# The stretch between two feed-forward blocks as one pipeline over tiles, with the window means as products on TensorE

## What is computed

```python
x = x + gate_f * rmsnorm_2(conv_ffn(h, w_up[0], ...), g_post_ffn[0])      # layer 0 ends
h = modulate(rmsnorm_2(x, g_pre_mix[1]), shift_m, scale_m)                # layer 1: h * (1 + scale) + shift
# multiscale_pool_mix: four groups of 256 channels, windows w = 2, 4, 8, 16 tokens
lo = jnp.clip(t - w // 2, 0, L); hi = jnp.clip(t + (w - w // 2), 0, L)
pooled = (csum[hi] - csum[lo]) / (hi - lo) - hg                           # window mean less the token itself
y = jnp.einsum('blgc,gce->blge', pooled, w_pool) + b_pool
y = y.reshape(B, L, D_MODEL) * pool_scale
x = x + gate_m * rmsnorm_2(y, g_post_mix[1])
h = modulate(rmsnorm_2(x, g_pre_ffn[1]), shift_f, scale_f)                # input of the second conv_ffn
```

## Time and profile before

| | |
|---|---|
| median of 3 runs | 4270.84 us (4269.49 to 4272.86) |
| the profiled execution's own time | 4271.75 us |
| its span, first to last instruction | 4269.8 us |
| mean granted TensorE clock | 0.914 of full speed |
| busy share: PE, PEld, DVE, ACT, POOL | 84%, 74%, 55%, 29%, 34% |

### The profile page before, as it was taken

How to read it: one execution, slowest core, us unless ns; L and a number is a source line. 1 busy time by engine, 2 the same in 40 slices (tenths; PEclk the granted TensorE clock), 3 DMA queues, 4 the chain that set the end, 5 groups by cost and what they waited for, 6 DMA issues and landing times. The chain is left out here.

```text
span 4269.8 us, 60179 instructions
## 1 busy us (share of the span) xinstructions
PE 3587.3 (84%) x19351; PEld 3162.1 (74%) x19351; DVE 2357.5 (55%) x4928; ACT 1228.9 (29%) x2747; POOL 1443.9 (34%) x1814
## 2 busy tenths in 40 slices
PE   5899877999998876757997769999994239999996
PEld 4799666999998865647886658888883238888885
DVE  6477664666777753126775244445445764444545
ACT  2255112656554521103432131112112022111111
POOL 3354322555665434431111342222213352222221
PEclk8899878999999978878998879999997569999998
DMA  4210544111111141100000021111101111111112
GB/s 163 80 39 17 222 182 156 39 40 58 56 58 54 33 170 49 40 11 1 0 0 30 10 99 44 59 44 44 45 28 40 40 69 59 53 50 44 44 44 79
DMA packets 67132, 255.69 MB, mean 60 GB/s; under 512 B 7328, under 2 KB 34208, under 8 KB 53920
## 3 DMA queue, kind: packets, MB, share of 16 engines
q1 hardware_dynamic: 66976, 253.79, 16.6%
HBM read 219.95 MB, written 33.82 MB: 59 GB/s over the span
## 5 line engine op out<-in xcount | busy, mean ns | idle before, releaser
L1777 PE MATMUL ps<-hT_hi,up_hi 128*128 128x512 f32 x1408 | 549.7, 390 | 15.0 <-DVEq L1730 15.0
L1778 PE MATMUL ps<-hT_lo,up_hi 128*128 128x512 f32 x1408 | 549.2, 390 | 0.0
L1779 PE MATMUL ps<-hT_hi,up_lo 128*128 128x512 f32 x1408 | 548.9, 390 | 0.0
L1681 POOL TENSOR_TENSOR up_lo<-up_raw,up_hi 128x2048 fp32r<-128x2048 f32 x42 | 194.5, 4630 | 866.6 <-ACT up_hi L1702 866.6
L1740 DVE TENSOR_TENSOR x<-ps,x 128x512 f32<-128x512 f32 x704 | 457.1, 688 | 2.1 <-PE ps L1793 2.1
L293 PE MATMUL ps<-w_hi,hT_hi 128*128 128x512 f32 x848 | 337.4, 398 | 70.2 <-DVE hT_lo L317 35.0
L294 PE MATMUL ps<-w_lo,hT_hi 128*128 128x512 f32 x848 | 335.6, 396 | 0.0
L295 PE MATMUL ps<-w_hi,hT_lo 128*128 128x512 f32 x848 | 335.3, 395 | 0.0
L545 PE MATMUL ps<-identity,rows 128*128 128x128 f32 x464 | 104.2, 417 | 273.3 <-DVE rows L441 254.8
L1777 PEld LDWEIGHTS ps<-hT_hi,up_hi 128*128 128x128 f32 x1408 | 265.2, 188 | 70.9 <-POOLq L1629 15.8
L1779 PEld LDWEIGHTS ps<-hT_hi,up_lo 128*128 128x128 f32 x1408 | 265.2, 188 | 55.3
(11 more groups left out here) (233 smaller groups left out, 8376.8 us busy)
## 6 DMA issues: line engine op xcount, KB each, us to landing
mod_weights<-in_w_mod SPq DMA_DIRECT2D x24, 2048.0 KB, 8.4
up_raw<-in_w_up SPq DMA_DIRECT2D x44, 1024.0 KB, 4.8
down_raw<-in_w_down SPq DMA_DIRECT2D x44, 512.0 KB, 5.6
w_raw<-in_w_in_b SPq DMA_DIRECT2D x24, 768.0 KB, 4.4
x_kept<-x SPq DMA_DIRECT2D x3, 4096.0 KB, 15.7
group_rows<-unit_rows SPq DMA_DIRECT2D x64, 132.0 KB, 1.8
unit_rows<-group_rows SPq DMA_DIRECT2D x64, 132.0 KB, 2.1
x<-in_x SPq DMA_DIRECT2D x2, 4096.0 KB, 15.6
```

What stands on the lines that cost most here:

```text
L1777: nc.tensor.matmul(out, a, t_hi[:, k, cols], start=(k == 0), stop=False)
L1778: nc.tensor.matmul(out, a, t_lo[:, k, cols], start=False, stop=False)
L1779: last = nc.tensor.matmul(out, b, t_hi[:, k, cols], start=False, stop=(k == KT - 1))
```

## The change

All blocks listed above, from the residual of layer 0 to the columns of the second `conv_ffn`, become one block, `PoolMix`, written out over 22 slots. In slot i an engine handles tile i - lag for each of its steps, so that up to eight tiles are in flight at different steps. The lags on VectorE are: scale with 1/rms (1), add the old row (2), scaled rows `h` (3), copy of half the pooled columns (6), scale of the mixed rows (8), residual (9), normed rows (11), `lo` columns (13).

The window means become products: for a tile and a group of 128 channels TensorE multiplies the tile's own rows with a 128x128 band matrix (the inverse counts, less the identity), and adds the last 64 rows of the tile before and the first 32 rows of the tile behind, with matrices from a new input `windows`. The result comes out with channels on the partitions, which is what the product with `w_pool` wants; the first `turn` is gone. The bias is a float32r product over 64 partitions (bias `hi` in row 0, `lo` in row 32, zeros elsewhere), `pool_scale` is multiplied into `w_pool` once. The mean of squares goes to ScalarE (Identity with scale 1/1024 and bias eps), so GpSimd has one small instruction per 1/rms and not two. Shift and gain of the last turn are one ScalarE instruction per 128 columns (eight a tile); the shift of `h` stays a GpSimd add. The factors and rows that were made by `rows_of_product` and `gained` are made once, after the second mixer, by `keep_rows`: seven small instructions of VectorE, one transpose, one copy, one DMA to a DRAM tensor, from which each is loaded by a broadcasting DMA. `X` is stored to `x_kept` tile by tile. Both `conv_ffn` are unchanged, and so is all before them.

```diff
+class PoolMix:
+    SLOTS = TILES + 14
...
+    def sync(self, sp):
+        sp.dma_start(self.old[:, 0], self.kept[:, 0]).then_inc(core.ready0.sem, 16)
+        sp.dma_start(self.old[:, 1], self.kept[:, 1]).then_inc(core.ready1.sem, 16)
+        sp.wait_ge(core.row_vectors.sem, core.row_vectors.at(16))
+        sp.dma_start(self.f_post[:], self.rows[0].partition_broadcast(P)).then_inc(core.post_row.sem, 16)
+        for dst, row in ((self.p_row, self.rows[1]), (self.s_row, self.rows[2])):
+            sp.dma_start(dst[:], row.partition_broadcast(P)).then_inc(core.pre_rows.sem, 16)
+        for dst, src in ((self.B[:], I["windows"]), (self.w[:], I["w_pool"]), (self.e_row[:], I["pool_scale"].partition_broadcast(P)),
+                         (self.b_row[:], I["b_pool"].partition_broadcast(P)), (self.f_mix[:], self.rows[3].partition_broadcast(P))):
+            sp.dma_start(dst, src).then_inc(core.constants.sem, 16)
+        self.ahead.first_loads(sp)
+        for m in range(2, TILES):
+            sp.wait_ge(core.x_new.sem, core.x_new.at(m - 1))
+            sp.dma_start(self.old[:, m % 2], self.kept[:, m]).then_inc((core.ready0, core.ready1)[m % 2].sem, 16)
+        for m in range(TILES):
+            sp.wait_ge(core.x_next.sem, core.x_next.at(m + 1))
+            sp.dma_start(self.kept[:, m], self.X[:, m]).then_inc(core.x_kept.sem, 16)
...
+    def tensor(self, pe):
+        for i in range(self.SLOTS):
+            m = self.tile_at(i, 6)
+            if m is not None:
+                if m == 0:
+                    pe.wait_ge(core.constants.sem, core.constants.at(16 * 5))
+                pe.wait_ge(core.h_rows.sem, core.h_rows.at(min(m + 2, TILES)))
+                for half, used in ((0, core.pooled_act), (1, core.pooled_dve)):
+                    pe.wait_ge(used.sem, used.at(m))
+                    for k in range(4 * half, 4 * half + 4):
...
+                        last = nc.tensor.matmul(out, H[:, m % 5, cols], B[:, g, 0 if m == 0 else 2 if m == TILES - 1 else 1],
+                                                start=True, stop=not (before or behind))
+                        if before:
+                            last = nc.tensor.matmul(out, H[P // 2:P, (m - 1) % 5, cols], B[P // 2:P, g, 3], start=False, stop=not behind)
+                        if behind:
+                            last = nc.tensor.matmul(out, H[0:P // 4, (m + 1) % 5, cols], B[0:P // 4, g, 3], start=False, stop=True)
+                    last.then_inc(core.pooled.sem, 1)
+            m = self.tile_at(i, 11)
...
+            m = self.tile_at(i, 7)
...
+                    nc.tensor.matmul(bank, self.one[:], self.bias[:, half * 512:half * 512 + 512], start=True, stop=False)
+                    for g in (2 * half, 2 * half + 1):
                         for k in range(2):
...
+                            last = nc.tensor.matmul(bank[:, (g % 2) * 256:(g % 2) * 256 + 256], self.d[:, m % 2, 2 * g + k], self.w[:, g, k],
+                                                    start=False, stop=(k == 1 and g % 2 == 1))
...
+        def square(n, m, src):
...
+            act.activation(self.junk[:, len(used) % 2], src, ACT.Square, accum_out=self.ss[:, n, m:m + 1]).then_inc(done[n].sem, 1)
...
+            act.activation(self.rs[:, n, m:m + 1], self.ss[:, n, m:m + 1], ACT.Identity, scale=1.0 / D, bias=core.eps[:]).then_inc(mean[n].sem, 1)
...
-        feed_forward(0)
...
-            turn(core, TILES, Stage(core, x_rows(X)), scale=pre[:], shift=mod[1][:, 0:8], plain=h)
-            pool_windows(core, h, I["inverse_counts"])
...
+                pool_mix(PoolMix(core, st2, T, T_at, up_at, X, x_dram, rows_dram, I, pre_ffn[:], mod[1][:, 24:32], up_weights))
+            feed_forward(1, T, up_weights)
```

More of the change, by code:

```diff
@@ L2043, in rows_of_product @@
     core.turned.passed(1)
[L2048 to L2104, removed]
@@ L2142, with pool_mix @@
+def pool_mix(mix):
+    with mix.core.nc.Block() as block:
+        block.sync(mix.sync)
+        block.gpsimd(mix.gpsimd)
+        block.scalar(mix.scalar)
+        block.vector(mix.vector)
+        block.tensor(mix.tensor)
+    mix.passed()
 VECTORS = {}
@@ L2363, in build @@
-        if stop == "e":
-            return ended()
-        feed_forward(1, lambda m: out[0, m * P:(m + 1) * P, :])
+        with ExitStack() as st:
+            T = split_columns(st)
+            gained(core, pre[:], vcol("g_pre_ffn", 0), mod[0][:, 32:40])
+            up_weights = UpWeights(core, st, I["w_up"][0])
+            turn(core, TILES, Stage(core, x_rows(X)), T, scale=pre[:], shift=mod[0][:, 24:32], ahead=up_weights, kept=(x_dram, X[:]))
+            feed_forward(0, T, up_weights)
+        with ExitStack() as st:
+            T_at = nc.sbuf_base
+            T = split_columns(st)
+            up_at = nc.sbuf_base
+            up_weights = UpWeights(core, st, I["w_up"][1])
+            with ExitStack() as st2:
+                pool_mix(PoolMix(core, st2, T, T_at, up_at, X, x_dram, rows_dram, I, pre_ffn[:], mod[1][:, 24:32], up_weights))
+            feed_forward(1, T, up_weights)
@@ L2368, in tile_part @@
+        with ExitStack() as st:
+            factor = core.sb(st, "factor", [P, D])
+            rows_of_product(core, vcol("g_post_ffn", 1), mod[1][:, 40:48], factor[:])
+            add_normed(core, x_tile, factor[:], x_tile, old=lambda m: x_dram[:, m], result=lambda m: out[0, m * P:(m + 1) * P, :])
 def tile_part(Z):
@@ L2416, in constants @@
     masks = np.stack([np.where(np.stack(p, 1), f(0), f(BIG)) for p in pairs]).astype(f)
[L2417 to L2420 removed]
+    windows = np.zeros((4, len(t), len(t)), f)
+    for g, w in enumerate((2, 4, 8, 16)):
+        lo, hi = np.clip(t - w // 2, 0, len(t)), np.clip(t + w - w // 2, 0, len(t))
+        inside = (t[:, None] >= lo) & (t[:, None] < hi)
+        windows[g] = np.where(inside, f(1) / (hi - lo).astype(f), f(0)) - np.eye(len(t), dtype=f)
+    first, mid, last = ((m * P, (m + 1) * P) for m in (0, 1, TILES - 1))
+    beside = np.zeros((4, P, P), f)
+    beside[:, P // 2:] = windows[:, P + P // 2:2 * P, 2 * P:3 * P]
+    beside[:, :P // 4] = windows[:, 2 * P:2 * P + P // 4, P:2 * P]
+    windows = np.stack([windows[:, a:b, a:b] for a, b in (first, mid, last)] + [beside], 1).transpose(2, 0, 1, 3)
+    return {"rotary": rotary, "axial": axial, "masks": masks, "windows": windows,
             "identity": np.eye(P, dtype=f)}
```

328 lines of the change are left out of this document (270 added, 58 removed).

## The result

The changed kernel takes **4205.4 us** (median of 4 runs, 4197.5 to 4208.3) against 4271.3 for the kernel before (median of 4 runs beside it): a ratio of 0.984 with a 95% interval of 0.983 to 0.986. It is 66 us faster. The prediction was 4146, 125 faster, with a range up to 4186. The sign was right, and the time lies 19 us above the range.

What follows compares the result with a forecast made beforehand. No engine was full; the chain of blocks bounded the stretch. Filling 27, TensorE 97.6, emptying 19, block ends 1.2 and `keep_rows` 5 made 149.8 against 274.6 us, so 4270.84 - 124.8 = 4146.0 us, range 4122 to 4186.

Steps and rivals of the forecast that it cites:

- The bare work: TensorE's products and transposes for the eight tiles of the new block, at full clock: 74.7 us.
- The changes of height: TensorE switching between products over 128, 64 and 32 rows: 192 changes at 0.08 us, 15.4 us (0 to 31.3).
- Half clock: TensorE starting its phase at half clock after being idle: some 2.5 us.
- Rival (d): TensorE stays at half clock through its phase, 180.3 us in place of 97.6: total 4229 us; chance 0.13.
- Waits of the first tiles: In TensorE's phase, first tiles wait for each other, as window products need the tile behind: 5 us.
- (b): Each change of height on TensorE breaks the overlap in full, 31.3 us: 16 more, total 4162 us; chance 0.14.
- Filling: Start of the stretch until TensorE's first product, behind 7.5 MB of queued transfers: 27 us.
- Emptying: The last mixed tile's way through the remaining steps to the end: 19 us, middle of 14.3 and 24.
- Rival (c): VectorE and GpSimd hold each other up, pace 13.1 us a tile: 11 more, total 4157 us; chance 0.14.
- Rival (e): Slots don't overlap as written; an in-order loop lets one tile through per 22.6 us: total 4229 us; chance 0.05.
- (a): No change of height on TensorE costs anything and the tail is bare: total 4126 us; chance 0.10.
- (f): At half clock each change of height also exposes a weight load, 0.61 us each: slower, 4315 us; chance 0.02.

Runs made afterwards that it cites:

- experiment 1: The changed kernel with all window and bias products over 128 rows, missing rows filled with zeros: 4143.2 us, ratio 0.970.
- experiment 8: The kernel of experiment 5 with VectorE's small product for the low part of the bias row one slot earlier: 4130.3 us, ratio 0.967.
- experiment 3: The changed kernel with its 128, 64 and 32 rows kept but window products grouped by height, 72 changes: 4155.3 us (one run).
- 4: The changed kernel with the three window products of every second channel group in reverse order, 130 changes of height: 4170.4 us, ratio 0.977.
- experiment 5: The kernel of experiment 1 with old rows of all eight tiles in own buffers, tiles 2 and 3 loaded before the constants: 4134.8 us, ratio 0.969.

## Why the prediction was wrong, step by step

**The step that failed** is the TensorE sum, 74.7 + 15.4 + 2.5 + 5 = 97.6, in its second and third terms.

- *The bare work*, 74.7, held: 75.5 busy us in experiment 1.
- *The changes of height*, 15.4, were mis-sized. I took 0.08 for each, the middle of 0 and 0.163, "as no row is nearer to either end". Measured are 0.19 at full clock, 188 of them 35.7 us, so 20 more. The upper end was too low as well: 0.163 is a product's own duration less its spacing, and the step takes 0.03 longer than that. What a step consists of was not shown. The Trainium skill, *TensorEngine Tiling (Array Packing)*, Key Properties, says that a change of the tiling mode drains TensorE; the spacing agrees with that rule, and my middle value went against it.
- *Half clock*, 2.5, "at the start" only, was the larger miss. With 74.7 + 35.7 = 110.4 us at full clock and none waiting, the other 37.7 of the 148.1 are the clock. They fit the two levels: all at half clock would be 144.6 + 188 x 0.30 = 201, so 42% of the work ran at half clock, which gives a mean of 0.72 where the row reads 0.69. The first 31.6 us of the phase ran at 0.50, and a part of each of the next tiles. Rival (d) argued the clock from gaps between products, and I gave it 0.13 because there would be no gap. There was none in the rows (148.08 busy of 148.10), and the clock fell all the same, so "unbroken work" in the sense of these rows is not enough to hold it up. At a change of height the rows show no gap either: a pair lasts 0.48 us and the next starts 0.41 after it, where pairs of one height last 0.39 and stand 0.22 apart. The time of the change is inside what counts as busy.
- *Waits of the first tiles*, 5, were nil in the kernel after, because everybody is faster than a slow TensorE. With a fast TensorE, experiment 1, they came to 10 us (85.6 less 75.5), of which 6.8 are the bias row, a wait I had not seen; without it, experiment 8, they are the 5 I put.

(b) and (d) were priced as rivals apart. They have one cause (experiments 1, 3 and 4) and came together, the one in full and a bit more, the other for 42% of the work. 20 + 35 less 5 for the waits make the 50.5 that the phase was over.

**The other steps.** *Filling* 27, measured 28.0; the queue of transfers was the cause, as argued, and experiment 5 confirms it. *Emptying* 19, measured 24.4 without the block ends, the upper of my two ends (24): I had left out that transposes and column scaling alternate over the same two banks, 5.02 us a tile, that TensorE is at half clock there (eight transposes 1.94 us, not 0.9), and that ScalarE's eight take 2.90 us, not 2.2. *`keep_rows`* 5, measured 3.4. *VectorE and ScalarE hidden*: right, at 57.7 and 46.3 busy of 148.1. *Rival (c)*: its mechanism is there, and off the path but for the filling (1.35 us); GpSimd's shift took 3.03 on average in the stretch (24.2 us for eight). The Trainium skill, *SBUF — State Buffer*, SBUF: two separate sides, describes the shared port pair as an exclusive lock, and the 3.25 us pairs of experiment 5 agree with it. *Rival (e)* is refuted by experiment 1, where the same slots, with the same waits between them, run at 85.6 us for eight tiles; (e) asked for 181. *Rivals (a) and (f)* fall by the spacing: a change costs neither 0 nor 0.61. The transfer term of the filling is 22.8 by the prediction's own rate (15.2 us for 5 MB), not 22; 22.1 was measured.

Experiment 1 landed on 4143, close to my 4146, but this is no confirmation of the sum: it has no change of height, and 10 us of waits in their place. That the two numbers meet is luck.

## What to carry to other kernels

Count how often consecutive products on TensorE differ in the number of rows, and not only how many columns they stream: here padding with zeros to 128 rows did more arithmetic in the same streaming time and gave back 62 us, and merely grouping equal heights gave 50 (one run). A TensorE that is "busy" 100% can be losing time between heights, so take the spacing of products, and price a new pattern with its clock, since both effects can have one cause. When a bottleneck is removed, look in each engine's ordered list for what its slowness had covered (a one-row bias here), and put shared work only where the engine that takes it isn't ahead of the bottleneck with something else.

## What the runs showed of the hardware

- A change between float32 products of 128 columns over 128, 64 and 32 rows costs 0.19 us at full clock and 0.30 at half, in each direction. The profile counts that time as busy.
- Eight equal products over 64 or 32 rows stream as fast as eight over 128 (0.112 us each in experiment 3).
- With 188 such changes in 148 us the granted clock went to and fro between 0.50 and 1.00 once a tile, down in the window products and up in the products with `w_pool`, 0.69 on average, though TensorE's rows leave no gap. With 72 in 97 us it was 0.50 for the first 24.4 us and 1.00 from then on. With none and a wait of 6.8 us in the phase it was 0.94, without that wait 0.98.
- A VectorE add of two SBUF operands takes 1.22 us alone and 3.25 beside an add on GpSimd, and GpSimd's, 1.9 alone, takes 3.25 then.
